# Hybrid GLA/MoBA decoder layer on one core: split waits for the high and low weight halves, gate evictions behind the splits, modulation units two slots further ahead

## What is computed

```python
mod = silu(c) @ w_ada + b_ada                        # (2048) x (2048, 12288), six vectors
h = rmsnorm(x, g_pre_mix) * (1 + sc1) + sh1
proj = h @ w_in                                      # widths: GLA q,k,v,gate,rank-16; MoBA q,k,v; two gates of 2048
y_a = gla(...) @ w_gla_out;  y_b = moba(...) @ w_moba_out
y = (sigmoid(gate_a) * y_a + sigmoid(gate_b) * y_b) @ w_o
x = x + gt1 * rmsnorm(y, g_post_mix)
h = rmsnorm(x, g_pre_ffn) * (1 + sc2) + sh2
up = causal_conv3(h @ w_up) + b_conv                 # 2048 -> 11264
u, g = split(up)
x = x + gt2 * rmsnorm((gelu(g) * u) @ w_down, g_post_ffn)
```

## Time and profile before

| | |
|---|---|
| median of 3 runs | 1526.21 us (1525.96 to 1538.2) |
| profiled execution | 1526.64 us, span of its core 1524.8 us |
| busy | PE 95%, weight loads 81%, DVE 73%, ACT 49%, POOL 6% of the span |
| HBM read | 364.18 MB |
| chain that ended last | PE 83%, DVE 6%, DMA 5%, issue 2%, ACT 2% |

### The profile page before, as it was taken

How to read it: one execution, slowest core, us unless ns; L and a number is a source line. 1 busy time by engine, 2 the same in 40 slices (tenths; PEclk the granted TensorE clock), 3 DMA queues, 4 the chain that set the end, 5 groups by cost and what they waited for, 6 DMA issues and landing times.

```text
span 1524.8 us, 19960 instructions
## 1 busy us (share of the span) xinstructions
PE 1451.1 (95%) x7386; PEld 1239.4 (81%) x7386; DVE 1109.2 (73%) x1117; ACT 754.3 (49%) x745; POOL 84.4 (6%) x176
## 2 busy tenths in 40 slices
PE   2898989999999999999989999999999999999996
PEld 1777878888888888877768888888888888888885
DVE  6878868889898987865487777777777666555554
ACT  3443343445354546433466656656665665444442
POOL 3000001111111110000000000000000000000000
PEclk9899989999999999999979999999999999999998
DMA  9988958898988976867547767677675555555552
GB/s 362 353 298 318 331 179 278 298 282 287 285 293 273 292 267 229 299 236 253 175 144 235 239 226 239 204 232 238 226 241 192 186 182 194 190 197 188 198 188 102
DMA packets 235526, 367.03 MB, mean 241 GB/s; under 512 B 11455, under 2 KB 161473, under 8 KB 234706
## 3 DMA queue, kind: packets, MB, share of 16 engines
q1 hardware_dynamic: 215536, 294.69, 57.9%
q0 software_dynamic: 18848, 69.23, 12.8%
q10 hardware_dynamic: 1090, 2.40, 0.4%
HBM read 364.18 MB, written 2.10 MB: 240 GB/s over the span
## 4 chain that ended last, share of the span: by engine, by line
PE 83%; DVE 6%; DMA 5%; issue 2%; ACT 2%; POOL 1%; SPq 0%; DVEq 0%; POOLq 0%
PE ps L1139 82%; DMA ada<-in_w_ada 2%; DVE acc L706 2%; DVE lo L696 2%; DMA raw<-in_w_in 1%; ACT hi L426 1%; DMA raw<-in_w_o 1%; DVE acc_a L725 1%; DMA raw<-in_w_moba_out 0%; DMA raw<-in_w_down 0%; POOL maskf L380 0%; DMA raw<-in_w_up 0%; DVE acc_b L725 0%; SPq L261 0%; POOL maskf L382 0%
## 5 line engine op out<-in xcount | busy, mean ns | idle before, releaser
L1139 PE MATMUL ps<-hT,hi 128*128 128x512 f32 x1936 | 467.2, 393 | 1.7 <-DVE hT L1051 1.7
L1139 PEld LDWEIGHTS ps<-hT,hi 128*128 128x128 f32 x1936 | 357.4, 189 | 73.1 <-issue 3.0
L426 ACT ACTIVATE hi<-raw 128x2048 fp32r<-128x2048 f32 x117 | 223.9, 1914 | 262.5 <-DMA raw<-in_w_in 162.0
L696 DVE TENSOR_TENSOR lo<-raw,hi 128x2048 fp32r<-128x2048 f32 x117 | 267.3, 2286 | 83.9 <-ACT hi L426 83.8
L1139 PEld LDWEIGHTS ps<-hT,lo 128*128 128x128 f32 x1936 | 248.2, 191 | 9.4
L1139 PE MATMUL ps<-hi,hT 128*128 128x512 f32 x768 | 248.7, 401 | 4.1 <-DVE hT L752 4.1
L1139 PE MATMUL ps<-hT,lo 128*128 128x256 f32 x1936 | 251.1, 283 | 0.0
L1100 DVE TENSOR_TENSOR lo<-raw,hi 128x2048 fp32r<-128x2048 f32 x88 | 200.1, 2291 | 49.8 <-ACT hi L657 49.6
L1139 PE MATMUL ps<-hi,asp 128*128 128x512 f32 x704 | 218.4, 391 | 2.3 <-DVE lo L696 2.3
L1139 PEld LDWEIGHTS ps<-hi,hT 128*128 128x128 f32 x768 | 148.4, 193 | 35.9 <-DVE lo L696 4.2
L657 ACT ACTIVATE hi<-raw 128x2048 fp32r<-128x2048 f32 x88 | 166.3, 1907 | 4.2 <-DMA raw<-in_w_up 3.3
(11 more groups left out here) (196 smaller groups left out, 1341.5 us busy)
## 6 DMA issues: line engine op xcount, KB each, us to landing
raw<-in_w_up SPq DMA_DIRECT2D x176, 512.0 KB, 4.4
raw<-in_w_in SPq DMA_DIRECT2D x162, 512.0 KB, 5.3
ada<-in_w_ada POOLq DMA_DIRECT2D x128, 512.0 KB, 4.8
raw<-in_w_down SPq DMA_DIRECT2D x88, 512.0 KB, 4.1
adar<-in_w_ada SPq DMA_DIRECT2D x64, 512.0 KB, 8.3
raw<-in_w_o SPq DMA_DIRECT2D x32, 512.0 KB, 4.7
raw<-in_w_gla_out SPq DMA_DIRECT2D x16, 512.0 KB, 4.8
raw<-in_w_moba_out SPq DMA_DIRECT2D x16, 512.0 KB, 5.5
```

What stands on the lines that cost most here:

```text
L426: act.activation(hi[:, w % 4, :], raw[:, w % 4, :], ACT.Copy).then_inc(hi_done, 1)
L696: dve.tensor_tensor(lo[:, w % 4, :], raw[:, w % 4, :], hi[:, w % 4, :].bitcast(F32), ALU.subtract).then_inc(lo_done, 1)
L1139: return pe.matmul(out_, lhsT, rhs, start=start, stop=stop)
```

## The change

Three edits.

1. TensorE starts a window when `hi_done` has it and waits for `lo_done` only ahead of the matmuls that use `lo`. For that, `tokens_still` and `one_row_tile` run all products with `w_hi` first and those with `w_lo` last; `weights_still` had that order. The number of matmuls is the same.
2. In the head loop, for windows below `W_LOW`, the eviction of window w - 1 now stands in iteration w behind the split of w + 3 (`gate_out`), on ScalarE and on VectorE, instead of the eviction of w ahead of it. From w = 25 on nothing moves on VectorE.
3. SyncE issues four units instead of two after the loads of windows 2 and 3, and so from then on each unit two windows earlier: after the load of window w, units 2w + 20 and 2w + 21 instead of 2w + 16 and 2w + 17. Buffers stay eight.

```diff
--- before.py
+++ after.py
@@ -302,7 +302,7 @@
                 else:
                     q, s = gate_at(w)
                     load_grid(w, win, 4 * q, 4, C_GA + 512 * GATE_CB[q][s], 512)
-                for _k in range(2):
+                for _k in range(4 if w in (2, 3) else 2):
                     if u < 4 * KT:
                         load_unit(u)
                         u += 1
@@ -470,19 +470,22 @@
             for w in (1, 2):
                 split_hi(w)
 
+            def gate_out(w):
+
+                q, s = gate_at(w)
+                if w != W_LOW and gate_copied(q, s):
+                    cb, pair = GATE_CB[q][s], GATE_PAIR[q][s]
+                    act.wait_ge(used, w + 1)
+                    act.activation(GA[:, cb // 4, :, 512 * (cb % 4):512 * (cb % 4 + 1)], ps[:, 2 * pair:2 * pair + 2, :],
+                                   ACT.Copy).then_inc(gate_copy, 1)
+
             for w in range(W_HEAD):
-                if w != W_LOW:
-                    q, s = gate_at(w)
-                    cb = GATE_CB[q][s]
-                    if gate_copied(q, s):
-                        pair = GATE_PAIR[q][s]
-                        act.wait_ge(used, w + 1)
-                        act.activation(GA[:, cb // 4, :, 512 * (cb % 4):512 * (cb % 4 + 1)], ps[:, 2 * pair:2 * pair + 2, :],
-                                       ACT.Copy).then_inc(gate_copy, 1)
-                else:
+                split_hi(w + 3)
+                if w == W_LOW:
                     act.wait_ge(used, w + 1)
                     act.activation(galow_x[0:RANK, :], ps[0:RANK, 7, TOK:], ACT.Copy).then_inc(low_x, 1)
-                split_hi(w + 3)
+                elif w and w < W_LOW:
+                    gate_out(w - 1)
...
@@ -799,7 +802,8 @@
                 level_decay(I, 0)
                 level_decay(I, 1)
 
-            for w in range(W_HEAD):
+            def gate_out(w):
+
                 q, s = gate_at(w)
                 if w != W_LOW and not gate_copied(q, s) and not gate_stays(q, s):
                     cb, pair = GATE_CB[q][s], GATE_PAIR[q][s]
@@ -807,11 +811,18 @@
                     dve.wait_ge(used, w + 1)
                     dve.wait_ge(gate_copy, copies_through(min(q, 1), 7))
                     dve.tensor_tensor(g, g, ps[:, 2 * pair:2 * pair + 2, :], ALU.add).then_inc(gate_add, 1)
+
+            for w in range(W_HEAD):
+                q, s = gate_at(w)
+                if w > W_LOW:
+                    gate_out(w)
                 if w == W_LOW:
                     link(dve.memset(galow[0:32, :], 1.0))
                     dve.wait_ge(low_x, 1)
                     dve.tensor_tensor(galow[0:RANK, :], ps[0:RANK, 7, 0:TOK], galow_x[0:RANK, :], ALU.add).then_inc(low_ready, 1)
                 split_lo(w + 3)
+                if 0 < w < W_LOW:
+                    gate_out(w - 1)
...
@@ -1138,38 +1149,43 @@
             def mm(out_, lhsT, rhs, start=True, stop=True):
                 return pe.matmul(out_, lhsT, rhs, start=start, stop=stop)
 
-            def weights_still(k, acts, k0, kn, bank, done, before=None):
+
+            def weights_still(k, acts, k0, kn, bank, remainders, before=None):
                 for j in range(8):
                     if before:
                         before(k0 + j)
                     for ct in range(2):
                         mm(ps[:, bank + ct, :], hi[:, k, 256 * j + P * ct:256 * j + P * (ct + 1)], acts[:, k0 + j, :], k0 + j == 0, False)
+                pe.wait_ge(lo_done, remainders)
                 for j in range(8):
                     for ct in range(2):
                         ins = mm(ps[:, bank + ct, TOK:], lo[:, k, 256 * j + P * ct:256 * j + P * (ct + 1)], acts[:, k0 + j, 0:TOK],
                                  False, k0 + j == kn - 1)
-                ins.then_inc(done, 1)
-
-            def tokens_still(k, acts, k0, bank, first, last, before=None):
+                return ins
+
+            def tokens_still(k, acts, k0, bank, first, last, remainders, before=None):
 
                 for j in range(4):
                     if before:
                         before(k0 + j)
                     for tt in range(TT):
-                        a_hi_, a_lo_ = acts[:, k0 + j, P * tt:P * (tt + 1)], acts[:, k0 + j, TOK + P * tt:TOK + P * (tt + 1)]
-                        w_hi, w_lo = hi[:, k, 512 * j:512 * (j + 1)], lo[:, k, 512 * j:512 * (j + 1)]
-                        mm(ps[:, bank + tt, :], a_hi_, w_hi, first and j == 0, False)
-                        mm(ps[:, bank + tt, :], a_hi_, w_lo, False, False)
-                        ins = mm(ps[:, bank + tt, :], a_lo_, w_hi, False, last and j == 3)
+                        w_hi = hi[:, k, 512 * j:512 * (j + 1)]
+                        mm(ps[:, bank + tt, :], acts[:, k0 + j, P * tt:P * (tt + 1)], w_hi, first and j == 0, False)
+                        mm(ps[:, bank + tt, :], acts[:, k0 + j, TOK + P * tt:TOK + P * (tt + 1)], w_hi, False, False)
+                pe.wait_ge(lo_done, remainders)
+                for j in range(4):
+                    for tt in range(TT):
+                        ins = mm(ps[:, bank + tt, :], acts[:, k0 + j, P * tt:P * (tt + 1)], lo[:, k, 512 * j:512 * (j + 1)], False, last and j == 3)
                 return ins
 
-            def one_row_tile(k, acts, first, last_, tt, blocks=range(4)):
+            def one_row_tile(k, acts, first, last_, tt, remainders, blocks=range(4)):
                 a_hi_, a_lo_ = acts[:, P * tt:P * (tt + 1)], acts[:, TOK + P * tt:TOK + P * (tt + 1)]
                 for b in blocks:
-                    w_hi, w_lo = hi[:, k, 512 * b:512 * (b + 1)], lo[:, k, 512 * b:512 * (b + 1)]
-                    mm(ps[:, 4 * tt + b, :], a_hi_, w_hi, first, False)
-                    mm(ps[:, 4 * tt + b, :], a_hi_, w_lo, False, False)
-                    ins = mm(ps[:, 4 * tt + b, :], a_lo_, w_hi, False, last_)
+                    mm(ps[:, 4 * tt + b, :], a_hi_, hi[:, k, 512 * b:512 * (b + 1)], first, False)
+                    mm(ps[:, 4 * tt + b, :], a_lo_, hi[:, k, 512 * b:512 * (b + 1)], False, False)
+                pe.wait_ge(lo_done, remainders)
+                for b in blocks:
+                    ins = mm(ps[:, 4 * tt + b, :], a_hi_, lo[:, k, 512 * b:512 * (b + 1)], False, last_)
                 return ins
 
...
@@ -1219,13 +1236,13 @@
...
-                pe.wait_ge(lo_done, w + 1)
+                pe.wait_ge(hi_done, w + 1)
...
-                tokens_still(w % 4, hT, 4 * q, 2 * GATE_PAIR[q][s], fresh, q == 3 or not gate_stays(q, s),
+                tokens_still(w % 4, hT, 4 * q, 2 * GATE_PAIR[q][s], fresh, q == 3 or not gate_stays(q, s), w + 1,
                              h_is_ready if s == 0 else None).then_inc(used, 1)
...
```

More of the change, by code:

```diff
@@ L1211, in _ @@
                         mm(ps[:, 7, :], hi[:, w % 4, P * k:P * (k + 1)], hT[:, k, :], k == 0, False)
+                    pe.wait_ge(lo_done, w + 1)
                     for k in range(KT):
@@ L1295, in _ @@
                             pe.wait_ge(evac, 5 * (G // 5) + {0: 2, 1: 3, 2: 4, 4: 5}[G % 5])
-                    pe.wait_ge(lo_done, w + 1)
+                    pe.wait_ge(hi_done, w + 1)
                     if g == 3:
-                        tokens_still(w % 4, hT, 4 * (n - 6), b, n == 6, n == 9).then_inc(used, 1)
+                        tokens_still(w % 4, hT, 4 * (n - 6), b, n == 6, n == 9, w + 1).then_inc(used, 1)
                     else:
-                        weights_still(w % 4, hT, 8 * (n % 2), KT, b, used)
+                        weights_still(w % 4, hT, 8 * (n % 2), KT, b, w + 1).then_inc(used, 1)
                     if I:
@@ L1363, in _ @@
                 pe.wait_ge(oo_ready, branch + 2 * half + 1)
-                pe.wait_ge(lo_done, w + 1)
-                tokens_still(w % 4, og_om, 4 * branch + 8 * half, merge_bank(cb, branch), half == 0, half == 1).then_inc(used, 1)
+                pe.wait_ge(hi_done, w + 1)
+                tokens_still(w % 4, og_om, 4 * branch + 8 * half, merge_bank(cb, branch), half == 0, half == 1, w + 1).then_inc(used, 1)
                 tail(HEADS - 1, m)
@@ L1376, in _ @@
                 k = (W_WO + kt) % 4
-                pe.wait_ge(lo_done, W_WO + kt + 1)
+                pe.wait_ge(hi_done, W_WO + kt + 1)
                 pe.wait_ge(mt_ready, kt // 4 + 1)
@@ L1382, in _ @@
                 if kt < 3:
-                    one_row_tile(k, mT[:, kt, :], kt == 0, False, 0)
+                    one_row_tile(k, mT[:, kt, :], kt == 0, False, 0, W_WO + kt + 1)
                 if kt == 0:
@@ L1394, in _ @@
                     pe.wait_ge(mt_ready, 4)
-                    one_row_tile(W_WO % 4, mT[:, 0, :], True, False, 1, (2, 3))
+                    one_row_tile(W_WO % 4, mT[:, 0, :], True, False, 1, W_WO + 1, (2, 3))
                     pe.wait_ge(g_ready, 2)
-                    one_row_tile(W_WO % 4, mT[:, 0, :], True, False, 1, (0, 1)).then_inc(used, 1)
```

(28 more changed lines are left out.)

## The result

The changed kernel takes 1554.32 us (median of 4 runs, 1551.55 to 1559.09) against 1527.3 for the kernel before in the same runs. The ratio is 1.0163, 95% interval 1.0138 to 1.0189: slower by 1.6%. The prediction was 1537, range 1521 to 1550: the measured time lies outside. The side on which the change falls and the place were forecast, the size was not.

A forecast was written before the change was run, and what follows sets the result against it. TensorE was taken as the bound, busy 95% of the span, idling mainly in the head before the sums. 1526.64 + 14.9 (head loads held) - 4.5 (split waits), late evictions 0, gave 1537 us, range 1521 to 1550.

The forecast's parts named there:

- the hold: Head, SyncE's queue: each window load waits behind units of iteration w - 4, a two-window loop of 13.4 us; head +14.9 us.
- the wait does not hold the queue: Rival, head: real loop is 11 us or less, only the split waits' gain is seen, 1522 us; chance 0.11.
- the faster one: Rival, head: the three stalls at the sums and the slow stretch behind them go, 1501 us; chance 0.07.
- the first leg of a turn: Head loop, from a window load's issue to ScalarE's start on it: taken as 6.5 us, between 5.58 and 7.45.
- The third quarter: Head, third sums: two loops of 13.4 + 1.2, then two VectorE-limited iterations of 5.93 each; start at 209.8 against 194.88 us.
- second legs: Head loop, from ScalarE's start to the end of the second unit: 6.8 us, and 0.1 for SyncE.
- the free middle waits: Some 300 more waits in the middle of TensorE's windows: taken to cost zero.
- The estimate from the Trainium skill: Head loop: load to ScalarE's start 5.5 us, loop 12.4, head +7, time 1529; the trace's 387 GB/s spoke against it.
- the loop holds harder than a turn of 14.35: Rival, head: the two-window load loop exceeds its upper bound, DMA queue refilling behind each stall, above 1550 us; chance 0.05.
- The rival of the middle waits: Rival, TensorE's windows: each of 300 added waits costs 0.05 us, 15 us more, 1552 us; chance 0.06.

The follow-up runs named there:

- one slot: Changed kernel with three units instead of four after the loads of windows 2 and 3, so units run one place further ahead, not two: 1523.61 us, ratio 0.9963.
- twelve buffers: Changed kernel with four more unit buffers from unit 24 on, same order on SyncE's queue: 1524.15 us, ratio 0.9970.
- units_first2: Kernel before with split waits, and both splits of iterations 4 and 5 (12 and 13, 20 and 21) behind the quarter's last four units: 1512.34 us, ratio 0.9885.

## Why the prediction was right or wrong

- **Right: the hold and its place.** The loads stand behind the pair, the chain shows the loop, and the kernels with edit 3 undone, with it alone, with one slot and with twelve buffers all agree. The rival "the wait does not hold the queue" (0.11) and the faster one (0.07) fall for this change.
- **Wrong: the first leg of a turn, taken as 6.5 us, upper bound 7.45.** In the changed kernel the loads of windows 4 to 17 (without that of 11, in front of which no pair had just left) take 6.8 to 9.7 us from issue to ScalarE's start, 8.1 in the mean. The six legs on the path in quarters 1 and 2 (windows 4, 6, 8, 12, 14, 16) add up to 48.1 us where the sum has 39.0. That is 9.1 of the 15.1 us by which the head is longer than forecast (30.0 against 14.9). The step that failed is the sentence that put the leg between the two rows because the queue is "not full but never empty", and the upper bound from a single row of the kernel before. The same trace had longer legs: the load issued at 80.13 took 8.26 us, and those of windows 14 to 17 took 7.8 to 8.1:

```profile
88.39 1.91 ACT L426 ACTIVATE hi<-raw 128x2048 fp32r<-128x2048 f32 x1 [4.33 <-DMA raw<-in_w_in]
```

- **What the runs showed in its place:** fewer bytes stand in front, but they move more slowly. The rows of one stretch (columns as above), changed kernel and kernel before:

```profile
55.00:75.00 20.00, 17.75 (x78) 14.05 (x77) 12.81 (x9) 5.74 (x5) 0.00 (x0) 1.00 0.87 292
```

```profile
55.00:75.00 20.00, 20.00 (x90) 16.57 (x89) 17.20 (x11) 9.56 (x8) 0.00 (x0) 1.00 1.03 370
```

  In the leg of window 6 itself (70.0 to 77.7 us) it is 284 GB/s; in that of window 8 in the kernel before (74.7 to 82.1 us), from which the 7.45 came, 381. By the experiments half a MB less in front takes 2.2 us off, and the whole pair moved behind the load 2.5 in the mean. Why the transfers run more slowly behind a held pair stays open.
- **The third quarter took another path.** The sum has two turns and then two iterations with VectorE as the limit. The chain of the changed kernel goes from the held load of window 21 (first row) to the add for window 17 behind its split, to window 20 on TensorE, which waited 3.9 us for that add (second row), to the load of window 24 (third row) and the sums:

```profile
189.78 8.24 DMA raw<-in_w_in
...
203.47 7.39 PE ps L1150 x24
211.29 5.53 DMA raw<-in_w_in
```

  From the second sums to the third it is 60.3 us where the sum has 57.1, another 3.2 us, and a late eviction is on the path.
- **The remaining 2.8 us:** the load of window 4 left at 55.87, not 54.9; the six second legs of quarters 1 and 2 are 1.3 us longer together than counted (7.3 instead of 6.9 us where a load follows); the load of window 12 left 0.5 us later.
- **From the head to the time.** Of the 17.3 us between 1537 and 1554.3, the trace has 14.5: 15.1 in the head, less 0.6 elsewhere. The other 2.8 are the distance of the profiled execution (1551.55, the fastest of the four) from the median.
- **Right: edit 1**, -4.5 us forecast, 0.28% measured alone, and the free middle waits. TensorE's timeline of the changed kernel has no wait left at the end of `w_o` or of down.
- **Right: edit 2** at about nothing, alone. Behind held loads it makes the sums 0.7, 1.1 and 3.3 us later than edit 3 alone has them, where the prediction counted 0, 1.2 and 3.6 for the adds.
- **The estimate from the Trainium skill** ("DMA: Bandwidth & Descriptors", section "Anatomy of one DMA") was a leg of 5.5 us and a time of 1529. The page gives its fit for transfers that GpSimd issues, and SyncE issues these. The trace does not agree with the estimate: the leg was 8.1 us in the mean and the time 1554; the measurement decides.
- **The chances.** Slower had 0.28, though the forecast itself lay 0.3% from that border. With a leg of 8.1 us in its sum the forecast is 1550. The rival "the loop holds harder than a turn of 14.35", above 1550, had 0.05 and is the one that came: the six turns of quarters 1 and 2 took 14.0 to 16.6 us, 15.3 in the mean. The reason it gives, the queue refilling behind each stall, fits the lower GB/s, but no run isolates it. The rival of the middle waits (1552) lies near the measured time too; edit 1 alone rules it out.

## What to carry to other kernels

Before a transfer is moved ahead on an in-order queue, ask what it waits for, and what stands behind it: a prefetch that runs as far ahead as it has buffers turns every load behind it into part of a loop with the consumer. Close that loop on paper and divide by the windows that it spans; one slot less, or buffers for it, takes it away, and the edge is sharp. A leg of such a loop that no row shows needs a wide upper bound, at the least the longest of all similar rows and not one of them. And if one engine waits for the last of many small pieces of work, look first at what stands in front of that piece in its own engine's order, not at its data.

## What the runs showed that was not expected

- Between 55 and 195 us the changed kernel's transfers ran at 268 GB/s with a DMA share of 0.81. Per share that is 331 GB/s, against 354 in the kernel before (322 at 0.91). So the larger part of the lower rate is a lower busy share, the smaller one a lower rate while busy; neither was explained.
- In `units_first2` the sums of one-column matmuls run at 115 ns each (16 in 1.84 us) with no wait ahead of them, at a granted clock of 1.00 (86 to 89 us). In the changed kernel they run at 223 ns (3.57 us) after a wait of 7.76 us, at the lower of the two clocks (0.50 granted from 102 to 105 us, and 0.51 and 0.50 in the wait ahead from 99 to 102 us).
